# A decoder layer: products of the output projection are planned with twice as much attention beside each

## The reference

```
h    = rms_norm(x, norm_pre_mix);  proj = h @ w_in          # split into q, k, v, qi, ki, wi, hq, hf, hi, hg
score[t, s] = sum_h wi[t, h] * relu(qi[t, h] . ki[s])       # causal; top 256 keys of each query
att  = softmax(q . k over the chosen keys) @ v              # 8 heads of 64, 2 key/value heads
hg_out = gated linear recurrence (HGRN2) of hq, hf, hi, hg
mix  = concat(att, hg_out) @ w_out                          # the output projection
x    = x + rms_norm(mix, norm_post_mix)
h2   = rms_norm(x, norm_pre_ffn)
ff   = (silu(h2 @ w_gate) * (h2 @ w_up)) @ w_down           # width 2816
out  = x + rms_norm(ff, norm_post_ffn)
```

## Time and profile before

| | |
|---|---|
| median of three executions | 3402.47 us |
| the profiled execution, device time | 3398.05 us |
| its span, first to last instruction | 3396.3 us |
| TensorE busy | 3232.0 us (95%) |
| VectorE busy | 2248.5 us (66%) |
| ScalarE busy | 1499.6 us (44%) |
| GpSimd busy | 227.1 us (7%) |
| mean granted TensorE clock | 0.982 of full speed |

### The profile page before, as it was taken

One profiled execution on the slowest core, in us unless ns is written; L12 is line 12 of the kernel. 1 busy time (PEld: TensorE's weight loads), 2 busy tenths in 40 slices (PEclk: granted clock), 3 DMA queues, 4 the chain that ended last, 5 costly groups with the idle time before them and its releaser, 6 DMA issues.

```text
span 3396.3 us, 46669 instructions
## 1 busy us (share of the span) xinstructions
PE 3232.0 (95%) x18176; PEld 2852.3 (84%) x18176; DVE 2248.5 (66%) x3721; ACT 1499.6 (44%) x2477; POOL 227.1 (7%) x400
## 2 busy tenths in 40 slices
PE   8999999999888899999989999998999999989998
PEld 8999999999767688888778888887888888878886
DVE  3467677778555776666787677767876865463444
ACT  3454445455354544444455444445554444333222
POOL 0000000000110200010101001011000000010000
PEclk9999999999899999999999999999999999999999
DMA  5543443343221322222332222224211112252233
GB/s 182 167 127 126 131 146 108 128 141 129 97 85 68 111 74 83 78 86 72 139 122 71 71 75 74 66 89 164 70 67 62 55 61 72 90 186 96 90 104 108
DMA packets 147501, 345.75 MB, mean 102 GB/s; under 512 B 15056, under 2 KB 35920, under 8 KB 145232
## 3 DMA queue, kind: packets, MB, share of 16 engines
q1 hardware_dynamic: 144976, 338.55, 29.9%
q10 hardware_dynamic: 2304, 4.20, 0.3%
HBM read 283.38 MB, written 59.31 MB: 101 GB/s over the span
## 4 chain that ended last, share of the span: by engine, by line
PE 63%; DVE 5%; ACT 2%; issue 2%; DMA 1%; POOL 0%; DVEq 0%; SPq 0%; ACTq 0%; POOLq 0%
PE PJ_d L2040 9%; PE PJ_d L2042 9%; PE PJ_d L2041 9%; PE SC L2000 6%; PE PJ_d L2065 6%; PE PJ_d L2067 6%; PE PJ_d L2066 6%; PE SA L1959 4%; PE SA L1960 3%; PE SA L1986 3%; PE SA L1955 1%; DVE wd_lo L1800 1%; DVE prob L1785 1%; DVE h_lo L1805 1%; ACT h_hi L1566 0%
## 5 line engine op out<-in xcount | busy, mean ns | idle before, releaser
L2040 PE MATMUL PJ_d<-h_hi,wd_hi 128*128 128x512 f32 (+1 forms) x1472 | 577.6, 392 | 19.7 <-DVE h_lo L1805 17.7
L2042 PE MATMUL PJ_d<-h_hi,wd_lo 128*128 128x512 f32 (+1 forms) x1472 | 565.1, 384 | 0.0
L2041 PE MATMUL PJ_d<-h_lo,wd_hi 128*128 128x512 f32 (+1 forms) x1472 | 564.0, 383 | 0.0
L1556 ACT ACTIVATE wd_hi<-wd_raw 128x512 fp32r<-128x512 f32 x568 | 344.7, 627 | 232.1 <-DMA wd_raw<-in_w_gu 132.8
L720 PE MATMUL PJ<-w_hi,h_hi 128*128 128x338 f32 (+1 forms) x1280 | 416.3, 325 | 2.8 <-DVE w_lo L546 2.8
L1551 ACT ACTIVATE pT<-SA 128x512 f32<-128x512 f32 (+3 forms) x320 | 156.7, 532 | 587.7 <-PE SA L1986 587.7
L1800 DVE TENSOR_TENSOR wd_lo<-wd_raw,wd_hi 128x512 fp32r<-128x512 f32 x568 | 380.1, 688 | 50.3 <-ACT wd_hi L1556 47.3
L721 PE MATMUL PJ<-w_lo,h_hi 128*128 128x338 f32 (+1 forms) x1280 | 409.0, 320 | 0.0
L722 PE MATMUL PJ<-w_hi,h_lo 128*128 128x338 f32 (+1 forms) x1280 | 408.9, 319 | 0.0
L1785 DVE CUSTOM_DVE_ANT_0 prob<-SA,bias 128x1024 f32<-128x1024 f32 (+7 forms) x192 | 170.1, 911 | 319.9 <-PE SA L1960 312.6
L2040 PEld LDWEIGHTS PJ_d<-h_hi,wd_hi 128*128 128x128 f32 x1472 | 281.2, 191 | 70.5 <-DVE h_lo L1805 11.3
(11 more groups left out here) (202 smaller groups left out, 5737.9 us busy)
## 6 DMA issues: line engine op xcount, KB each, us to landing
wd_raw<-in_w_gu SPq DMA_DIRECT2D x352, 256.0 KB, 2.8
wd_raw<-in_w_down SPq DMA_DIRECT2D x176, 256.0 KB, 2.6
w_raw<-in_w_in SPq DMA_DIRECT2D x40, 684.0 KB, 4.6
w_raw<-in_w_in SPq DMA_DIRECT2D x40, 676.0 KB, 4.5
row_h<-proj_d SPq DMA_DIRECT2D x16, 1024.0 KB, 7.1
proj_d<-stage SPq DMA_DIRECT2D x40, 342.0 KB, 4.3
proj_d<-stage SPq DMA_DIRECT2D x40, 338.0 KB, 5.1
x_d<-acc SPq DMA_DIRECT2D x24, 512.0 KB, 2.6
```

The source lines that it names most:

```text
L1556: s_.activation(w_hi[:, u % RING, :], w_raw[:, u % RING, :], ACT.Copy).then_inc(w_hi_ready, 1)
L2040: t.matmul(to[:, tok], w_hi[:, r, w], h_hi[:, c, tok], start=(c == 0 and part != 1), stop=False)
L2041: t.matmul(to[:, tok], w_hi[:, r, w], h_lo[:, c, tok], start=False, stop=False)
L2042: last = t.matmul(to[:, tok], w_lo[:, r, w], h_hi[:, c, tok], start=False, stop=(c == KD - 1 and part != 0))
```

## The change

In the windows s = 0, 1, 2 an "out" product counts as two shares, every other product as one. `each` becomes the window's weight over the number of shares, and the loop gives an "out" product twice `each`. No instruction is added or removed on the chip: the items keep their order and move to other slots. The window s = -1, which holds the first four "out" products, and the tail are planned as before.

```diff
--- before.py
+++ after.py
@@ -984,13 +984,18 @@
             last = FIRST - 1
         mine = [x[0] for x in items[done:last + 1]]
         beside = sum(BESIDE.get(x, 0) for x in mine)
-        each = (sum(weight[k] for k in window) - beside) / sum(x not in BESIDE for x in mine)
+        parts = [0 if x in BESIDE else 2 if x == "out" and s >= 0 else 1 for x in mine]
+        each = (sum(weight[k] for k in window) - beside) / sum(parts)
         so_far, spent = 0.0, 0.0
         for k in window:
             so_far += weight[k]
             first = done
-            while done <= last and spent + BESIDE.get(items[done][0], each) <= so_far + 1e-6:
-                spent += BESIDE.get(items[done][0], each)
+            while done <= last:
+                kind = items[done][0]
+                share = BESIDE.get(kind, each * (2 if kind == "out" and s >= 0 else 1))
+                if spent + share > so_far + 1e-6:
+                    break
+                spent += share
                 done += 1
             fills[k] = (first, done)
         assert done == last + 1
```

## The result

The changed kernel takes 3431.36 us (median of four, 3425.84 to 3434.41) against 3403.42 for the kernel before beside it: ratio 1.0079, interval 1.0062 to 1.0097, which is 28 us slower. The forecast was +21 (3423, range 3402 to 3441, slower 0.76). The profiled execution took 3432.04 us with a span of 3430.2; before 3398.05 and 3396.3.

What follows compares the result with a forecast made beforehand. VectorE's queue was taken to limit blocks 4, 8 and 12, TensorE elsewhere. Losses of 9 + 11 + 1 = +21 us on 3398.05 gave 3419; with medians 4.4 higher, 3423, range 3402 to 3441.

Steps and rivals of the forecast that it cites:

- rival of no change: Better spread output products halve VectorE's idle time in block 8, which then takes 98 us; total 3402 us; chance 0.14.
- the faster one: Tile chains get three to four heads, gap waits go and the search doesn't collide: -12 us, 3390; chance 0.08.
- The lower clock: TensorE at the lower clock through heads 0 to 4 of blocks 4, 8, 12: +66 us, 3460; chance 0.03.
- rule on transposes: Skill's rule that transposes don't count as clock activity like other matmuls; by it the thinned heads would run at 1.2 GHz.
- Heads 3 to 6 of block 8: Output products meet the late search: VectorE's work 59.3 us against TensorE's 38.0, so TensorE loses 22.6.
- the lead: At the end of heads 3 to 6 of block 8, TensorE runs ahead by next scores and a product: about 3 us.
- Block 4: Three up products leave; TensorE loses 21.3 us there against 19.8 before: +1 us.
- Block 8: Seven full products, 19 us, leave; TensorE's loss rises from 23.7 to 32.4 us: +9; the block shrinks about 10.
- nothing to 3 us a block, taken as nothing: ScalarE's wait for the previous group's stored output, with fewer products beside it; priced at zero as VectorE's finish moves later too.
- 1 for the rest: TensorE's loss in block 8 outside heads 0 to 6, taken as 1 us within the 32.4.
- Block 12: Six up products leave; TensorE loses 30.3 us there against 19.6 before: +11 us.
- Waits of the gap transposes under 5 us in all: Sign that the forecast is wrong, listed as an alternative to block 8 at 98 us or less.

Runs made afterwards that it cites:

- three kernels with one block changed: Double share for output products only in the window starting at block 8, 12 or 4, against the kernel before: 3417.87, 3417.50 and 3403.24 us.
- half share: Output products in windows s = 0, 1, 2 count half a share instead of one, against the kernel before: 3388.31 us, ratio 0.9962.
- both repairs: Changed kernel with the search started in head 0 of blocks 8 and 12, and ScalarE's first output copy of groups 1 and 2 one item later: 3418.71 us.
- later copy: ScalarE's first output-product copy of groups 1 and 2 one item later: 3418.99 us on the changed kernel, 3400.03 on the kernel before, 3382.10 with output products at 0.5 shares.
- early search: Changed kernel with the search starting in head 0 instead of head 3: in blocks 4, 8 and 12 3428.80 us; in blocks 8 and 12 only 3420.19.

## Why the prediction was right

**Sign and mechanism held.** TensorE's work is the same, the products left blocks in which it was not the limit, and they are paid almost in full elsewhere (2.46 us each, taken as 2.71). The three kernels with one block changed, and the half share, which goes the other way by the same rule and wins 12.6 us, show it. The rival of no change needed block 8 at 98 us (117.4 measured, 106.7 with both repairs); the faster one needed half of the 14.5 us of the earlier trace rows gone and nothing in their place, and the wait moved to the transposes of head 6. The lower clock asked for less than 0.7 over block 8: the rows show 0.87, and 1.00 in heads 3 and 4. Those heads still had three output products, 8 of TensorE's 17 busy us, and in the block 3 that the prediction looked at, products were more than half of the busy time. So neither tests the rule on transposes well; a stretch of head 5, in the last section, tests it better and speaks against it.

**That the number is so near is in part luck.** By medians the loss is 28 us against 21 forecast, but on the profiled executions it is 34 (3432.0 against the 3419 that the prediction gave for them) and by the blocks 37. Blocks 8 and 12 each cost 7 to 10 us more than forecast, and only the wide range and the cheaper products leave this inside.

**Heads 3 to 6 of block 8 were priced right**: 60.6 us predicted, 59.0 measured (19.88 + 39.14). The terms fit too: VectorE's work less the lead was to be 56.3 us and is 54.0, its idle time 4.3 and is 5.0. VectorE is busy 36.1 of 39.1 us in heads 5 and 6, so not quite without a gap. The wait before head 6 was to be 7 us or more; it is 6.75. **Block 4** was to be +1; it is -0.3 by the profiled executions and +0.9 by its own kernel, both within noise.

**Block 8 did not shrink by 10 us.** It was to end 9 us above its share and ended 19 above. Two terms were mis-sized:
- "nothing to 3 us a block, taken as nothing", for ScalarE's wait for the stored output. The prediction reasoned that VectorE's finish moves later too, and priced only ScalarE's wait, not what is queued behind it. ScalarE's wait did not grow, as the rows show; what went is TensorE's work beside it, and TensorE's waits are 6.33 and 7.48 us. Heads 0 to 2 took 38.7 us against 34.8 predicted. The later copy shows the price, 5.0 us in block 8, 3.9 in block 12, and 9 to 10 of 28 in the medians.
- "1 for the rest". Heads 0 to 6 and the total of 107 left 12 us for head 7; it took 19.7. The last gap's low part, still late, costs 2.64 us of idle time, and the clock is 0.74 over the head (0.50 from 1784 to 1794 us, row in the last section; TensorE was busy 7.4 us of these ten, so by an estimate about 3.7 us went there): half-width matmuls begin 0.21 us apart in its first half and 0.12 apart in its second, as these rows of TensorE show. That this head runs out of VectorE is read from the trace and was not tried alone.

```profile
1789.24 0.41 PE L2047 MATMUL PJ_d<-h_hi,wd_lo 128*128 128x256 f32 x1
1789.45 0.41 PE L2045 MATMUL PJ_d<-h_hi,wd_hi 128*128 128x256 f32 x1
...
1795.31 0.28 PE L2045 MATMUL PJ_d<-h_hi,wd_hi 128*128 128x256 f32 x1
1795.43 0.28 PE L2046 MATMUL PJ_d<-h_lo,wd_hi 128*128 128x256 f32 x1
```

**Block 12** was +11 and measured +18.4. Its heads 0 to 2 were not given a ScalarE wait; 3.9 us of the miss go with the later copy. The early search took 2.7 us off this block, but that collision was in the forecast. The rest of the miss has not been tried apart.

**A marker was badly chosen.** "Waits of the gap transposes under 5 us in all" was to speak against the forecast. They came to 4.4 us (the L2012 rows) while the forecast held: the wait for VectorE had gone to the probabilities' transposes. A marker should name the engine waited for, not the instruction that happens to wait.

The prediction gave the wrong section for one rule: the advice to interleave regimes stands in the Trainium skill (Perfetto Trace Analysis) under "Optimization Strategy". The runs do not follow it at this dose: spread further, the output products made the kernel 0.8% slower; drawn together to half a share, 0.4% faster, and together to a quarter, 0.2%.

## What to carry to other kernels

Before giving a kind of item more room, ask which engine sets the end of the stretch that the displaced work leaves: if it isn't the engine of that work, the stretch stays as long and the work is paid again elsewhere; and try the dose on both sides, since here 0.5, 1 and 2 shares gave 3388, 3402 and 3431 us. Where an engine's queue holds an instruction that waits for a DMA, price what is queued behind it and what the waiting engine has beside it, not its own wait: ScalarE stood no longer after the change than before it, but its 3.4 us became 6.3 us of TensorE once the products beside it were gone, and issuing that copy an item later took 12 us off the changed kernel and 6 to 9 off the half-share one.

## What was not expected of the hardware

Behind some idle stretches TensorE runs at the lower of its two levels, 1.2 GHz (granted clock 0.50), and what it has next takes nearly twice as long. Eight transposes take 1.94 us after 6.75 us of idle time and 1.97 after 2.12, against 1.06 after 0.56; sixteen value matmuls take 3.68 after 7.48 and 2.00 after 0.69. It is not the length of the last wait alone that decides. In block 8 of the changed kernel the clock stayed at 1.00 behind a wait of 1.70 us (the transposes of head 4), and was 0.50 behind one of 1.41 (products in head 5, some 3 us behind another stretch at 0.50). The longest stretch at 0.50, 1784 to 1794 us, had a wait of 1.91 us before it and one of 2.64 within. What does decide, these runs don't show.

```profile
1749.69 1.97 PE L2012 MATMUL SA<-ident,tile 128*128 128x128 f32 x8 [2.12 <-DVE tile L1869]
```

```profile
1749.69:1753.00 3.31, 2.95 (x13) 2.55 (x14) 2.46 (x3) 1.81 (x4) 2.34 (x3) 0.50 0.85 277
1753.50:1755.24 1.74, 1.18 (x10) 0.86 (x8) 1.14 (x2) 1.74 (x4) 0.73 (x2) 1.00 0.93 378
1784.00:1794.00 10.00, 7.36 (x35) 6.38 (x34) 5.00 (x7) 4.04 (x5) 1.50 (x1) 0.50 0.08 28
```

From 1749.69 to 1755.24 us TensorE ran nothing but transposes, and still the clock rose from 0.50 to 1.00 at about 1753.

What the lower level costs is more than the first instructions behind a wait. TensorE was busy at 0.50 for 3.0 us behind the wait of 6.75 and for 5.9 behind that of 7.48, so by an estimate (half of those times) these waits carry 1.5 and 3 us more than themselves. Added up over windows of 0.25 us, it was busy at that level for 11.9 us of block 8 before and 20.8 after, and for 10.2 and 17.9 of block 12. Half of the difference, about 4 us a block, is an estimate of what the clock added to the loss; no run tried it apart from the idle time.
